# Joining short TensorE groups in a fused decoder layer: two heads' scores, and transposes two fills at a time

## The reference

```
h = rmsnorm(x);  z = h @ w_in           -> q_lat, c_kv, k_pe, u_pool, gate_a, gate_p
y_a = mla(q_lat, c_kv, k_pe) @ w_attn_br         (16 heads, causal softmax, rotary part of 64)
y_p = pool(u_pool) @ w_pool_br
merged = sigmoid(gate_a) * y_a + sigmoid(gate_p) * y_p
x = x + rmsnorm(merged @ w_mix_out)
kv = rmsnorm(mem) @ w_mem_kv;  x = x + rmsnorm(softmax(q k^T) v @ w_mem_o)     (4 heads, 256 memory tokens)
x = x + rmsnorm((gelu(conv(h @ w_gate)) * conv(h @ w_up)) @ w_ffn_out)
```

## Time and profile before

| | |
|---|---|
| time, median of 3 runs | 1787.02 us (1786.98 to 1787.15) |
| the profiled execution: its own time | 1786.39 us |
| the profiled execution: span from first to last instruction | 1784.7 us |
| TensorE busy (matmul) | 1771.4 us, 99% of the span |
| TensorE weight loads busy | 1487.0 us, 83% |
| VectorE busy | 1171.0 us, 66% |
| ScalarE busy | 937.6 us, 53% |
| mean granted TensorE clock, as a share of full | 0.999 |

### The profile page before, as it was taken

One profiled execution on the slowest core, in us unless ns is written; L12 is line 12 of the kernel. 1 busy time (PEld: TensorE's weight loads), 2 busy tenths in 40 slices (PEclk: granted clock), 3 DMA queues, 4 the chain that ended last, 5 costly groups with the idle time before them and its releaser, 6 DMA issues.

```text
span 1784.7 us, 25258 instructions
## 1 busy us (share of the span) xinstructions
PE 1771.4 (99%) x8854; PEld 1487.0 (83%) x8854; DVE 1171.0 (66%) x1644; ACT 937.6 (53%) x1279; POOL 59.9 (3%) x128
## 2 busy tenths in 40 slices
PE   9999999999999999999999999999999999999998
PEld 7888888888887888888888878888888888888786
DVE  5555565655455655544555477777777777788887
ACT  7555565565545554444555474444444444455554
POOL 4000000000000110000000100000000000000002
PEclk9999999999999999999999999999999999999999
DMA  8555554554556555555444556555555555656565
GB/s 288 153 189 180 153 186 132 185 161 160 208 192 234 192 188 187 187 173 188 157 142 168 187 173 224 186 184 185 185 186 185 187 187 187 200 173 206 187 200 189
DMA packets 192239, 330.78 MB, mean 185 GB/s; under 512 B 17286, under 2 KB 43318, under 8 KB 190774
## 3 DMA queue, kind: packets, MB, share of 16 engines
q1 hardware_dynamic: 190630, 318.48, 54.0%
q10 hardware_dynamic: 1552, 11.54, 1.6%
HBM read 325.81 MB, written 4.19 MB: 185 GB/s over the span
## 4 chain that ended last, share of the span: by engine, by line
PE 97%; DVE 2%; ACT 1%; DMA 0%; issue 0%; DVEq 0%; ACTq 0%
PE bank L1030 17%; PE bank L588 15%; PE bank L590 15%; PE bank L589 15%; PE bank L1032 9%; PE bank L1078 4%; PE bank L1080 4%; PE bank L1079 4%; PE bank L896 3%; PE bank L897 2%; PE bank L758 2%; PE bank L759 1%; PE bank L620 1%; PE bank L781 1%; PE bank L783 1%; DVE wlo L1680 0%
## 5 line engine op out<-in xcount | busy, mean ns | idle before, releaser
L1680 DVE TENSOR_TENSOR wlo<-raw,whi 128x1024 fp32r<-128x1024 f32 x520 | 637.6, 1229 | 529.1 <-ACT whi L1189 378.9
L1189 ACT ACTIVATE whi<-raw 128x1024 fp32r<-128x1024 f32 x376 | 397.9, 1059 | 462.0 <-PE bank L590 246.4
L1030 PE MATMUL bank<-actA,whi 128*128 128x512 f32 x1344 | 472.0, 394 | 0.0
L1032 PE MATMUL bank<-actA,wlo 128*128 128x256 f32 x1344 | 380.1, 283 | 0.0
L1030 PEld LDWEIGHTS bank<-actA,whi 128*128 128x128 f32 x1344 | 252.4, 188 | 58.3
L588 PE MATMUL bank<-whi,actA 128*128 128x512 f32 x672 | 272.5, 405 | 1.6 <-DVE wlo L1680 0.7
L590 PE MATMUL bank<-whi,actA 128*128 128x512 f32 x672 | 265.3, 395 | 0.0
L589 PE MATMUL bank<-wlo,actA 128*128 128x512 f32 x672 | 265.0, 394 | 0.0
L1032 PEld LDWEIGHTS bank<-actA,wlo 128*128 128x128 f32 x1344 | 252.7, 188 | 0.0
L1175 ACT ACTIVATE whi<-raw 128x1024 fp32r<-128x1024 f32 (+1 forms) x144 | 150.5, 1049 | 138.8 <-PE bank L590 85.7
L588 PE MATMUL bank<-whi,actB 128*128 128x512 f32 x448 | 178.6, 399 | 0.5 <-DVE memk L1958 0.3
(11 more groups left out here) (289 smaller groups left out, 2064.9 us busy)
## 6 DMA issues: line engine op xcount, KB each, us to landing
raw<-in_w_ffn_in SPq DMA_DIRECT2D x88, 1024.0 KB
raw<-in_w_in SPq DMA_DIRECT2D x48, 1024.0 KB
raw<-in_w_ffn_out SPq DMA_DIRECT2D x84, 512.0 KB, 4.8
raw<-in_w_mem_kv SPq DMA_DIRECT2D x32, 1024.0 KB
raw<-in_w_attn_br SPq DMA_DIRECT2D x16, 1024.0 KB
raw<-in_w_mix_out SPq DMA_DIRECT2D x16, 1024.0 KB
raw<-in_w_mem_q SPq DMA_DIRECT2D x16, 1024.0 KB
raw<-in_w_mem_o SPq DMA_DIRECT2D x16, 1024.0 KB
```

Source lines behind the costliest of these rows:

```text
L1030: pe.matmul(dst[:, :], whi[:, s, o:o + P], actA[:, :, kt, :], start=(kt == 0), stop=False)
L1032: mm = pe.matmul(dst[:, 0:S], wlo[:, s, o:o + P], actA[:, 0, kt, :], start=False, stop=(kt == KD - 1))
L1189: act.activation(whi[:, ks % AHEAD, 0:w], raw[:, c, ks % 2, 0:w], ACT.Copy).then_inc(hi_done, 1)
L1680: dve.tensor_tensor(wlo[:, vs % AHEAD, 0:w], raw[:, c, vs % 2, 0:w], f32(whi[:, vs % AHEAD, 0:w]), ALU.subtract).then_inc(lo_done, 1)
```

## The change

On TensorE alone, `pair_job` now does the scores of both heads behind unit 0; `merged` does both its fills behind unit 2; `x2_job` does fills k and k + 1 behind units 0, 2, 4 and 6. `mem_job` does fills 0 and 1 behind unit 2 and fills 2 and 3 behind unit 4, and ScalarE's and VectorE's `mem_split` take them out in those same jobs. ScalarE's and VectorE's jobs of the other three places stay as they are.

```diff
-            if k in (0, 1):
-                if k == 0:
-                    pe.wait_ge(k_sum, 2 * i + 2)
-                    pe.wait_ge(at_out, f + 1)
-                for t in range(TT):
-                    w = (t + 1) * P
-                    dst = sc[k][:, t * P:t * P + w]
-                    pe.matmul(dst, qT[:, 2 * m + k, t * P:(t + 1) * P],
-                              bufX[:, m, bass.ds(i * NC + k * S, w)], start=True, stop=False)
-                    mm = pe.matmul(dst, qpeT[:, t * P:(t + 1) * P], kpeT[:, k, 0:w], start=False, stop=True)
-                mm.then_inc(s_filled, 1)
+            if k == 0:
+                pe.wait_ge(k_sum, 2 * i + 2)
+                pe.wait_ge(at_out, f + 1)
+                for h in range(2):
+                    for t in range(TT):
+                        w = (t + 1) * P
+                        dst = sc[h][:, t * P:t * P + w]
+                        pe.matmul(dst, qT[:, 2 * m + h, t * P:(t + 1) * P],
+                                  bufX[:, m, bass.ds(i * NC + h * S, w)], start=True, stop=False)
+                        mm = pe.matmul(dst, qpeT[:, t * P:(t + 1) * P], kpeT[:, h, 0:w], start=False, stop=True)
+                    mm.then_inc(s_filled, 1)
...
         def merged(n):
             def job(k):
-                if k in (2, 3):
+                if k == 2:
                     pe.wait_ge(mrg_ok, 2 * n + 2)
-                    t_fill(T_MRG + 2 * n + k - 2, k - 2, kch, 2 * (k - 2))
+                    for f in range(2):
+                        t_fill(T_MRG + 2 * n + f, f, kch, 2 * f)
...
         def mem_job(k):
-            for f in ((), (), (0,), (1,), (2,), (3,), (4, 5), (6, 7))[k]:
+            for f in ((), (), (0, 1), (), (2, 3), (), (4, 5), (6, 7))[k]:
...
         def x2_job(k):
-            pe.wait_ge(res_done, 8)
-            t_fill(T_X2 + k, k, bufX, 2 * k)
+            if k % 2 == 0:
+                pe.wait_ge(res_done, 8)
+                for f in (k, k + 1):
+                    t_fill(T_X2 + f, f, bufX, 2 * f)
...
         def mem_split(k):
-            for f in ((), (), (0,), (1,), (2,), (3,), (4, 5), (6, 7))[k]:
+            for f in ((), (), (0, 1), (), (2, 3), (), (4, 5), (6, 7))[k]:
```

## The result

The changed kernel takes 1789.26 us (median of 20 runs, 1789.05 to 1790.69) against 1786.98 us before (20 runs, 1786.62 to 1788.64): a ratio of 1.0013 with a 95% interval of 1.0007 to 1.0019, so 2.3 us slower (1.3 to 3.4). The forecast was 1787.8, with a range up to 1788.8. The sign was right, and the difference (0.13%) stays under the 0.2% that the forecast took for no change; but the loss is nearly three times what was forecast, and the time lies outside the range.

A forecast was written before the change was run, and what follows sets the result against it. The prediction took TensorE to bound the kernel. Its terms, -0.18 us from boundaries and +0.99 from the x2 column, summed to +0.8, giving 1787.8 us, with a range from 1786.4 to 1788.8.

The forecast's parts named there:

- What bounds the kernel: Whole kernel: TensorE, busy 1771.4 of 1784.7 us; only a shorter TensorE stream or TensorE waits can move the end.
- What a joined boundary gives: At 18 joined group boundaries on TensorE: 0.01 us saved each, 0.18 us in all, between 0 and 0.54.
- the rival of 3.0 us: At 18 boundaries: full matmul latency of 0.166 us each comes back, 1785.0 with the x2 wait; dear boundaries' chance 0.08.
- What the x2 column loses: x2 column: fills 3, 5 and 7 each wait 0.33 us for their bank, 0.99 us in all (0.66 without signal time).
- What costs nothing, `merged` and `mem_job`: Merged and memory fills: banks come free in time, no new wait; the 0.24 us at memory fills 6 and 7 stays.
- What costs nothing, the scores: Score groups: unit 1 ends 1.30 us later, VectorE still in time by 0.03 us; cost nothing, at most 0.5 us.
- The rival of the late normalising: L790, every pair: VectorE's head 0 normalising runs into weight work, delaying head 1's probabilities; up to 10.4 us; chance 0.05.
- The clock rival: Ten couples of transposes: longer runs drop the granted clock to 1.2 GHz, costing 8.7 us, 1796.5; chance 0.02.

The follow-up runs named there:

- Only the x2 couples: Kernel before with only the x2 column's fills done two at a time on TensorE: 1787.06 us against 1786.57, ratio 1.0004.
- The table loaded in time: Changed kernel plus one small exponential on ScalarE in job 0 of the second pairs: 1787.29 us against 1786.57 for the kernel before.

## Why the prediction was wrong

**What bounds the kernel:** right. TensorE's busy time stayed, and its waits carry the loss.

**What a joined boundary gives (0.18 us):** right that boundaries aren't dear, and the rival of 3.0 us is excluded. The pair of kernels with and without joins gives 0.1 us for sixteen, so no run shows even the 0.01 a boundary apart from nothing.

**What the x2 column loses (0.99 us):** right mechanism, right fills, right number of waits; mis-sized. It is 3 x 0.26 = 0.78 us. The signal took 0.06 us and not the 0.11 read at one memory fill. That lies within the stated 0.66 to 0.99. One side remark was a misreading on which nothing rests: before, a bank came free about one unit ahead of need and not two (fill 3 out at 754.23, fill 5 due at 750.86 + 2 x 3.23 = 757.32).

**What costs nothing, `merged` and `mem_job`:** right; no wait appeared and the 0.24 at fills 6 and 7 stayed.

**What costs nothing, the scores:** here it failed. The premise held, "The scores lengthen the way to unit 1: its end comes 1.30 us later, that of unit 2 stays"; the step that failed is the count of slack behind it, which ended in "I take nothing". It had two gaps. It followed only VectorE, on which the row maxima and normalisings lie, and never asked what ScalarE's job 1 does to ScalarE's own weight work in job 2. And it read rows of one pair, a first one, as if all eight were alike. For the first pairs the reading held to 0.01 us: VectorE's weight work follows the normalising without idle time and the waits stayed at 0.19. That hung on 0.03 us, so it was close. In second pairs ScalarE had 0.73 us to spare where 1.30 were needed. The waits there grew by 0.46 each, 1.8 us in all, where the sum had nothing.

With the terms as the runs found them, nothing from the boundaries, 0.78 from the x2 column and 1.9 at L790, the sum is +2.7 us: the profiled spans differ by that, the medians by 2.3 (1.3 to 3.4).

**The rival of the late normalising** named the right place, L790, and the right victim, head 1's probabilities, but not the cause. It asked for all pairs and looked for the delay on VectorE, where both ends were fixed by rows, so it got a chance of 0.05. Its sign, a wait at L790 of 0.3 or more, did come (0.65). The rows that would have priced it stood in the trace of before: the table load in front of the second pair's exponential, and the 0.73 us behind it.

**The clock rival** didn't happen: the granted clock was 1.00 over the x2 column with its couples (741 to 767 us) and over the eight pairs (185 to 455 us), 0.999 over the execution.

## What to carry to other kernels

When a group is moved ahead on one engine, walk through every engine that the next wait depends on and write down its idle time ahead of each step that shifts; the least of these decides, and it may be on an engine that does none of the moved work. Read it in every variant of the repeated place, not in the first one: here only every other pair had a table load in front of its exponential. On this stream, which was already gapless, joining short groups gave nothing that could be measured; what there was to win, 1.3 to 1.6 us, came from the order of the work on VectorE and from spreading the memory fills, with joins or without. Where groups are joined all the same, their takers must be moved with them, and no group may be moved ahead of its source.

## What the runs showed of the hardware

A lone group of four 128x128 float32 transposes between long matmuls costs 0.44 us and a couple 0.87, so the change of group is free to within 0.01 us at a granted clock of 1.00.

The exponential's table load takes 1.28 us on ScalarE. It stood directly in front of the exponential only where a sigmoid had run since the last load of the exponential's table: in the second pairs of the kernel before, and in the first pairs too once a sigmoid was added there. In first pairs of the kernel before it stood 26 us earlier, at the head of the round. A small activation of the same function, issued while ScalarE waits, moves the load into idle time at a cost of 0.20 us of ScalarE.

The granted clock can differ between executions at the start. In the profiled execution of "Only the x2 couples" it was 0.50 (the level of 1.2 GHz) from 12 to 14 us, and TensorE's unit matmuls took 0.43 us each, in place of 0.23, from 11.5 to 14.95 us. TensorE had been busy for 1.26 of the 2 us up to 11. In "The table loaded in time" it had been busy for 1.27 of them, and the clock stayed at 1.00; what makes the difference is not shown. The stretch lies ahead of everything that the edits touch. This execution took 1788.59 us, 1.5 above the median of its kernel.
